# First feed-forward block: all high parts of x ahead of the squares, and six units held unscaled in PSUM

## The reference, cut to what matters

```
def rms_norm(x, g):
    xf = x.astype(jnp.float32)
    y = xf * lax.rsqrt(jnp.mean(xf * xf, axis=-1, keepdims=True) + EPS)
    return (y * g.astype(jnp.float32)).astype(x.dtype)

def swiglu(x, w_gate, w_up, w_down):
    return (jax.nn.silu(x @ w_gate) * (x @ w_up)) @ w_down
...
        h = h + 0.5 * swiglu(rms_norm(h, ffn1_norm[l]), ffn1_w_gate[l], ffn1_w_up[l], ffn1_w_down[l])
```

## Time and profile before

| | us |
|---|---|
| three timed runs | 2091.92, 2092.68, 2093.68 (median 2092.68) |
| profiled execution, its own time | 2091.62 |
| its span | 2089.8 |
| TensorE matmuls busy | 1914.6 (92%) |
| VectorE busy | 1109.7 (53%) |
| ScalarE busy | 745.7 (36%) |
| POOL busy | 198.0 (9%) |

### The profile page before, as it was taken

How to read it: one execution, slowest core, us unless ns; L and a number is a source line. 1 busy time by engine, 2 the same in 40 slices (tenths; PEclk the granted TensorE clock), 3 DMA queues, 4 the chain that set the end, 5 groups by cost and what they waited for, 6 DMA issues and landing times.

```text
span 2089.8 us, 23172 instructions
## 1 busy us (share of the span) xinstructions
PE 1914.6 (92%) x8262; PEld 1500.9 (72%) x8262; DVE 1109.7 (53%) x1370; ACT 745.7 (36%) x1017; POOL 198.0 (9%) x176
## 2 busy tenths in 40 slices
PE   7999999999999999999896878989989979799996
PEld 5888778787666778888784556766766766578874
DVE  5444423337676554444224744744744734667874
ACT  4333322222445443333223332332332332456662
POOL 2000001103000010000002101001001001212231
PEclk9999999999999999999998789999999989899998
DMA  3232223323211223222222111221221221122333
GB/s 130 95 100 91 100 81 110 134 97 119 68 51 61 93 89 100 96 95 100 81 101 81 41 51 60 72 73 56 79 72 54 76 71 52 60 91 91 101 111 121
DMA packets 50054, 177.91 MB, mean 85 GB/s; under 512 B 5772, under 2 KB 6028, under 8 KB 50000
## 3 DMA queue, kind: packets, MB, share of 16 engines
q1 hardware_dynamic: 46944, 168.84, 24.4%
q0 software_dynamic: 1680, 6.04, 0.9%
q10 hardware_dynamic: 1376, 2.30, 0.3%
HBM read 172.97 MB, written 2.10 MB: 84 GB/s over the span
## 4 chain that ended last, share of the span: by engine, by line
PE 76%; DVE 11%; ACT 5%; issue 5%; POOL 2%; DMA 0%; DVEq 0%; ACTq 0%; POOLq 0%
PE banks L414 22%; PE banks L415 22%; PE banks L416 22%; ACT w_hi L795 3%; DVE w_lo L1162 1%; PE banks L684 1%; PE banks L546 1%; PE banks L577 1%; PE banks L531 1%; DVE rstd L1183 1%; DVE conv L1222 1%; POOL sumsq L1718 1%; POOL sumsq L1773 1%; PE banks L673 1%; PE banks L672 1%
## 5 line engine op out<-in xcount | busy, mean ns | idle before, releaser
L1162 DVE TENSOR_TENSOR w_lo<-w_raw,w_hi 128x1024 fp32r<-128x1024 f32 x317 | 397.2, 1253 | 793.0 <-ACT w_hi L795 792.0
L414 PE MATMUL banks<-u_hi,w_hi 128*128 128x512 f32 x1520 | 620.1, 408 | 65.0 <-DVE u_lo L1178 32.6
L415 PE MATMUL banks<-u_lo,w_hi 128*128 128x512 f32 x1520 | 603.2, 397 | 0.0
L416 PE MATMUL banks<-u_hi,w_lo 128*128 128x512 f32 x1520 | 602.3, 396 | 0.0
L795 ACT ACTIVATE w_hi<-w_raw 128x1024 fp32r<-128x1024 f32 x317 | 335.1, 1057 | 707.6 <-PE banks L416 630.7
L414 PEld LDWEIGHTS banks<-u_hi,w_hi 128*128 128x128 f32 x1520 | 292.5, 192 | 160.7 <-issue 37.8
L415 PEld LDWEIGHTS banks<-u_lo,w_hi 128*128 128x128 f32 x1520 | 293.1, 193 | 62.7 <-issue 4.2
L416 PEld LDWEIGHTS banks<-u_hi,w_lo 128*128 128x128 f32 x1520 | 291.9, 192 | 63.5
L1718 POOL TENSOR_TENSOR sumsq<-sumsq,sq 128x512 f32<-128x512 f32 x56 | 81.0, 1446 | 1015.8 <-ACT sq L804 1013.2
L414 PE MATMUL banks<-hid_hi,w_hi 128*128 128x512 f32 x352 | 141.1, 401 | 11.3 <-DVE hid_lo L1166 11.3
L415 PE MATMUL banks<-hid_lo,w_hi 128*128 128x512 f32 x352 | 140.6, 399 | 0.0
(11 more groups left out here) (244 smaller groups left out, 2259.1 us busy)
## 6 DMA issues: line engine op xcount, KB each, us to landing
w_raw<-weights SPq DMA_DIRECT2D x318, 512.0 KB, 3.3
bias<-neighbour_bias POOLq DMA_DIRECT2D x8, 384.0 KB, 4.5
x<-x_t ACTq DMA_DIRECT2D x4, 512.0 KB, 8.0
v_win<-v_a POOLq DMA_DIRECT2D x16, 128.0 KB, 2.7
out_t<-x SPq DMA_DIRECT2D x8, 256.0 KB, 2.1
rope<-rope_table POOLq DMA_DIRECT2D x1, 512.0 KB, 3.7
mask_b<-band_mask POOLq DMA_DIRECT2D x1, 192.0 KB, 3.4
vecs<-vectors ACTq DMA_DIRECT2D x1, 137.0 KB, 6.5
```

The source lines that it names most:

```text
L414: nc.tensor.matmul(o, wh, hi, start=start and k == 0, stop=False)
L415: nc.tensor.matmul(o, wh, lo, start=False, stop=False)
L416: ins = nc.tensor.matmul(o, wl, hi, start=False, stop=stop and k == len(pairs) - 1)
L1162: nc.vector.tensor_tensor(w_lo[:, n.slot, :], w_raw[:, n.slot, :], w_hi[:, n.slot, :].bitcast(F32), ALU.subtract)\
```

## The change

It touches `ffn` for the first block (f == 0) on three engines, and the start of ScalarE's program.

ScalarE makes u_hi of all eight chunks first, without waiting for POOL, and then the eight squares. Behind them it splits units 2 to 5, all ahead of rms. TensorE multiplies units 0 to 5 into banks 0, 1, 3, 4, 5 and 6 without waiting for a bank, with stat behind the fourth of them instead of behind the first. VectorE makes w_lo of units 2 to 5 before rstd, then reads the six banks as chunks 0 to 2, with the splits of units 6 and 7 ahead of gate and up of chunk 1. The loops then begin at chunk 3. The number of matmuls and of all other operations is the same.

```diff
--- before.py
+++ after.py
@@ -49,6 +49,7 @@
 U_WOUT = DC
 U_HEAD = 20
 U_PAIR = 8
+FFN1_HELD = (0, 1, 3, 4, 5, 6)
 U_FFN1 = 0
 U_MIX = U_FFN1 + U_FFN
 U_MERGE0 = U_MIX + U_QKV
@@ -446,11 +447,26 @@
                     pe.wait_ge(consts, 4)
                 nc.tensor.matmul(stat[:, :], ones[:, :], sumsq[:, :], start=True, stop=True).then_inc(stat_ready, 1)
 
+            def ffn_held():
+
+                for k, b in enumerate(FFN1_HELD):
+                    n = Lin(U_FFN1 + k)
+                    unit_ready(n)
+                    for c in range(DC):
+                        if k == 0:
+                            pe.wait_ge(u_lo_ready, c + 1)
+                        product(bank[b][:, :], [(c, u_hi[:, c, :], u_lo[:, c, :])], n, c == DC - 1, start=c == 0, stop=c == DC - 1)
+                    if k == 3:
+                        norm_stat(0)
+
             def ffn(f, q, nu, u0, g0):
-                first_unit(Lin(u0), Lin(g0), nu)
-                norm_stat(q)
-                linear8(Lin(u0 + 1), Lin(g0 + 1))
-                with pe.Fori(1, F_CHUNKS) as i:
+                if f == 0:
+                    ffn_held()
+                else:
+                    first_unit(Lin(u0), Lin(g0), nu)
+                    norm_stat(q)
+                    linear8(Lin(u0 + 1), Lin(g0 + 1))
+                with pe.Fori(3 if f == 0 else 1, F_CHUNKS) as i:
                     n, g = Lin(u0, 2, i), Lin(g0, 2, i)
                     linear8(n, g)
                     linear8(n + 1, g + 1)
@@ -811,9 +827,22 @@
                 nc.scalar.activation(rms[:, :], stat[:, :], ACT.Sqrt, bias=eps[:, 0:1], scale=1.0 / D).then_inc(rms_ready, 1)
 
             def ffn(f, q, q_next, nu_next, gcol, u0, g0):
+                if f == 0:
+                    for k in range(2, 6):
+                        split_raw(Lin(u0 + k))
                 norm_rms(q)
                 act.preload_act_table(ACT.Silu)
-                with act.Fori(0, F_CHUNKS) as i:
+                if f == 0:
+                    for c in range(3):
+                        if c == 1:
+                            split_raw(Lin(u0 + 6))
+                        act.wait_ge(bank_read, g0 + 2 * c + 3)
+                        nc.scalar.activation(gate_act[:, :], gate[:, :], ACT.Silu).then_inc(gate_acted, 1)
+                        if c == 1:
+                            split_raw(Lin(u0 + 7))
+                        act.wait_ge(hid_ready, c + 1)
+                        nc.scalar.activation(hid_hi[:, c, :], hid[:, :], ACT.Copy).then_inc(hid_hi_ready, 1)
+                with act.Fori(3 if f == 0 else 0, F_CHUNKS) as i:
                     n, g = Lin(u0, 2, i), Lin(g0, 2, i)
                     split_raw(n + 2)
                     act.wait_ge(bank_read, (g + 3).v())
@@ -836,7 +865,9 @@
             act.wait_ge(vec_loaded, 16)
             for m in range(DC):
                 act.wait_ge(x_loaded[m // 2], 16)
-                norm_chunk(0, Lin(m), 0, V_FFN1)
+                nc.scalar.activation(u_hi[:, m, :], x[:, m, :], ACT.Copy, scale=vecs[:, V_FFN1 + m:V_FFN1 + m + 1]).then_inc(u_hi_ready, 1)
+            for m in range(DC):
+                norm_chunk(0, Lin(m), None, 0)
             ffn(0, 0, 1, 1, V_MIX, U_FFN1, G_FFN1)
 
             norm_rms(1)
@@ -1189,8 +1220,26 @@
                                                ALU.mult, ALU.add).then_inc(bank_read, 1)
 
             def ffn(f, q, nu_next, gcol, u0, g0):
+                if f == 0:
+                    for k in range(2, 6):
+                        split_lo(Lin(u0 + k))
                 norm_rstd(q)
-                with dve.Fori(0, F_CHUNKS) as i:
+                if f == 0:
+                    for c in range(3):
+                        if c == 1:
+                            split_lo(Lin(u0 + 6))
+                        unit_done(Lin(u0 + 2 * c))
+                        nc.vector.tensor_tensor(gate[:, :], bank[FFN1_HELD[2 * c]][:, :], rstd[:, :], ALU.mult).then_inc(bank_read, 1)
+                        if c == 1:
+                            split_lo(Lin(u0 + 7))
+                        unit_done(Lin(u0 + 2 * c + 1))
+                        nc.vector.tensor_tensor(up[:, :], bank[FFN1_HELD[2 * c + 1]][:, :], rstd[:, :], ALU.mult).then_inc(bank_read, 1)
+                        dve.wait_ge(gate_acted, c + 1)
+                        dve.wait_ge(bank_read, g0 + 2 * c + 4)
+                        nc.vector.tensor_tensor(hid[:, :], gate_act[:, :], up[:, :], ALU.mult).then_inc(hid_ready, 1)
+                        dve.wait_ge(hid_hi_ready, c + 1)
+                        lo_part(hid_lo[:, c, :], hid[:, :], hid_hi[:, c, :]).then_inc(hid_lo_ready, 1)
+                with dve.Fori(3 if f == 0 else 0, F_CHUNKS) as i:
                     n, g = Lin(u0, 2, i), Lin(g0, 2, i)
                     split_lo(n + 2)
                     unit_done(n)
```

## The result

The changed kernel is slower: median 2097.64 us of 10 runs (2096.22 to 2099.49), against 2091.79 us of 10 runs of the kernel before in the same measurements (2089.09 to 2093.68). The ratio is 1.0031, 95% interval 1.0021 to 1.0041, that is +6.5 us (+4.4 to +8.6); the medians alone differ by 5.85. The forecast was 2099.5 for the median, 6.8 more than before. The profiled execution has 2097.49 us and a span of 2095.7 us, 5.9 more than before in both.

The account below looks back on a forecast made before the run. POOL paces the first unit and TensorE bounds everything from unit 6 on. Unit 6 starts 4.5 us later and the lower clock adds 2.3: +6.8 us, 2099.5 for the median (2098.4 profiled), range 2095.0 to 2103.3.

Parts of the forecast that it names:

- All u_hi first, squares behind them: Start of the first block: u_hi done at 13.5, POOL's additions from 14.2, unit 1 done near 23.6, unit 2 not ready.
- POOL's additions: First block's sum of squares: 1.36 us per addition, 0.3 for a collision; last square at 22.6, unit 2 at 26.4.
- The first idle time's clock: Ahead of unit 2 TensorE idles 2.8 us; the lower clock behind it loses 1.4 us, bounds 0 and 2.3.
- the rival in which the clock holds: Clock stays up through the first idle time: less 1.4, +5.4 us in all, 2098.1; chance 0.28.
- The chain behind stat: Serial operations from stat to unit 6 take 18.7 us; TensorE idles 6.8 us ahead of unit 6.
- The clock behind the second idle time: Behind TensorE's 6.8 us idle time ahead of unit 6 the clock is at its lower level: +2.3 us.
- The sum: Unit 6 at 57.4 instead of 52.9, +4.5 us, plus 2.3 for the clock: +6.8 us; chance 0.45.
- the two rivals in which it holds: Clock holds through the first idle time (+5.4 us, chance 0.28) or through both (+3.1 us, 0.12 with a like shortening).
- the slow ones: POOL's additions keep their 1.71 us, first idle time is 4.9 us: +9.8 us, 2102.5; chance 0.12.
- The bridged case: Units 2 and 3 ready at 23.6, short chain behind stat, TensorE never idles: unit 6 6.5 us earlier, 2086.2; chance 0.03.

## Why the prediction was right

- **All u_hi first, squares behind them.** As forecast: u_hi to 13.5, POOL from 14.07 (14.2), unit 1 done at 23.8 (23.6). With the units as before, this part alone costs 4.2 us.
- **POOL's additions.** That they run at 1.29 us busy was right, but two sizes in the sum of the last square were too small. The one collision with u_lo was taken at 0.3 us and cost 0.9 (2.21 instead of 1.29 for the first addition). And the additions start 1.44 us apart, as do the squares that wait for them (16.30 to 23.49), not the 1.36 that I took from another place: 0.3 over the four steps from the second to the sixth. The last square was 0.9 us late (23.49 against 22.6). w_lo of unit 2 took 2.27 us instead of 2.09, which adds 0.2: unit 2 at 27.42 instead of 26.4, 1.0 in all.
- **The first idle time's clock.** The clock fell, as it does behind the 3.07 us in the earlier trace rows; the idle time was 3.63 us instead of 2.8. Stat at 40.08 less two units of 5.44 from 27.42 leaves 1.8 us, where I had 1.4; with the idle time filled, the two units take 10.88 us and nothing of the 1.8 is left. But the length of an idle time alone doesn't tell what the clock does behind it, though the three rows that I had chosen look like that. In the kernel before, TensorE idles 1.83 us ahead of 1498.65 and 3.26 us ahead of 1545.29; the stretches behind these two are

```profile
...
1498.60:1502.80 4.20, 4.15 (x11) 0.59 0.36 125
1545.20:1549.40 4.20, 4.12 (x18) 1.00 0.38 125
...
```

So 1.83 us were followed by the lower clock once and 3.26 us were not, and that the term was near 1.4 and not 0 was in part luck; the rival in which the clock holds was a fair one.
- **The chain behind stat.** 18.69 us from stat to unit 6 against 18.7 worked out, the same in the kernel with the early splits. What made it count is one wait: `bank_free` counts all reads in order, so unit 6 waits for the fifth read though its bank was free after the first. Taking that wait to its own bank gave 8 us back.
- **The clock behind the second idle time.** 1.8 us by the filled idle time, 2.0 by the stretch from 58.7 to 63.0 (4.30 x 0.47); I had 2.3. What decides how long it stays low is open: 4.0 us here, 6.1 behind the same idle time in the kernel with the early splits.
- **The sum.** At the end of the gate and up units it is 7.8 us, against 6.8 forecast; 1.0 is POOL's additions and w_lo, 0.4 the first clock term, 0.3 less the second. At the end of the program 5.9 are left in the profiled execution and 6.5 by the ratio of the timed runs. So the sum at the end came out near the forecast partly by luck: the error of 1.0 was covered by 1.9 us that I had not counted and that came back later. Up to the end of the attention stage 1.2 are gone (a matmul behind it starts at 664.23 before and at 670.88 now), and 0.4 of them are there again at the last stores. 0.9 lie in the first 29 us of the attention stage, which have a different share of lower clock in the two executions, the kernel before and then the changed one:

```profile
...
500.60:530.00 29.40, 29.36 (x150) 0.91 0.20 65
...
```

```profile
...
508.20:537.60 29.40, 29.39 (x154) 0.94 0.23 78
...
```

29.4 x 0.03 is 0.9 us; why the clock differs there wasn't tested. Another 1.1 lie behind the last stored tile: SP's last issue ends 3.4 us before the end of the span in the kernel before, 2.3 in the changed one, and the longest of the eight last stores takes 3.4 us to land there, 2.2 here. The shift in time isn't what sets this: in all nine traces the longest landing is 3.3 to 3.4 us in the kernel before and in the one with u_hi first alone, and 2.2 in the seven that hold six units, whether they are earlier or later than before. What in those programs shortens it stays open; it is 1.1 us that is no work of the first stage.
- **The rivals.** The clock fell both times (0.87 and 0.53), which rules out the two rivals in which it holds, and POOL's additions took 12.21 us and not 13.7, which rules out the slow ones. The bridged case was refuted for this kernel by the two idle times, but its price was sound: with both obstacles removed and stat a unit earlier, TensorE has no pause, and unit 8 and all behind it come 6.9 us earlier (6.6 counted from the first matmul), where I had 6.5.

## What to carry to other kernels

Before the busiest engine gets work earlier, ask what feeds the work behind it: here POOL's additions and the last square set when the following weights were split, and they started 4 us later. An in-order count of freed buffers serves a two-buffer rhythm, but once buffers are filled out of it, each wait has to name the read of its own buffer. A pause of the matmul engine can cost more than its length: some 1.8 us behind each of the two here, though nothing behind the 3.26 us pause above.

## What the runs showed that I had not expected

The clock need not be at its lower level when matmuls resume, and can fall behind that: behind the 3.63 us the first four had 0.50 and 0.40 us and the long ones began 1.3 us later, while in the kernel with the filled second idle time the same pause, 4.17 us there (unit 1 ended sooner), was followed by a long first matmul (0.79 us). The loss came to nearly the same (stat 12.66 and 12.59 us behind the start of unit 2).

An addition of POOL and an operation of VectorE hold each other up, and which one is held depends on which comes first. In the changed kernel the last addition begins 0.08 us ahead of w_lo: it keeps 1.27 us, and w_lo goes from 1.23 to 2.27. In the kernel with the early splits w_lo of unit 2 (20.68, 2.31 us) is held by the addition ahead of it and then holds the next one:

```profile
...
22.05 2.08 POOL L1771 TENSOR_TENSOR sumsq<-sumsq,sq 128x512 f32<-128x512 f32 x1
...
```

The Trainium skill, SBUF — State Buffer, "SBUF: two separate sides", says that of such a pair (GpSimd, and VectorE with two inputs from SBUF) the one that starts first has the port pair that they share for the whole instruction and the other is blocked. The trace agrees in the order and nearly in the size: w_lo ends 1.08 us behind the addition that it waited for (27.36 against 26.28), where it takes 1.23 alone.
